# HGRN: who forms the second half of the scaled keys, GpSimd or VectorE

## The reference

```
def _gla_chunked(q, k, v, logf, s0):
    '''S_t = diag(f_t) S_{t-1} + k_t v_t^T, o_t = S_t^T q_t; q,k,logf [B,H,L,dk], v [B,H,L,dv].'''
    c = HGRN_CHUNK
    q, k, v, logf = (_chunks(t, c) for t in (q, k, v, logf))
    gc = jnp.cumsum(logf, axis=-2)
    ...
    attn = jnp.einsum('nbhid,nbhjd,nbhijd->nbhij', q, k, decay)
    ...
        o = qd_i @ s + a_i @ v_i
        s = s * gl_i[..., None] + jnp.einsum('bhcd,bhce->bhde', kd_i, v_i)
```

## Time and profile before

| | before |
|---|---|
| runs | 1703.83, 1696.02, 1699.45 us |
| median | 1699.45 us |
| time of the profiled execution | 1695.34 us |
| span of its profile | 1693.5 us, TensorE clock 0.921 of full speed in the mean |
| HGRN stage, state update ahead of it to the last one in it | 653 to 839 us |

### The profile page before, as it was taken

The page is one execution under the profiler, slowest core; times in us unless marked ns, Lnnn a source line. Parts: engine busy times, 40 slices in busy tenths (PEclk is TensorE's granted clock), DMA queues, the critical chain, the costliest instruction groups (busy, mean ns, idle before and its releaser), DMA issues. The chain is left out here.

```text
span 1693.5 us, 21841 instructions
## 1 busy us (share of the span) xinstructions
PE 1483.8 (88%) x8370; PEld 1087.4 (64%) x8370; DVE 727.8 (43%) x1234; ACT 424.3 (25%) x788; POOL 313.8 (19%) x395
## 2 busy tenths in 40 slices
PE   4999999996999997778679649788999999999955
PEld 1566876754898885444435534476888888888721
DVE  2612670166655654666752630343322222222246
ACT  3111000215555553333232000133221222122101
POOL 0100000103212111344310211101111111111154
PEclk9989789897999998899877769889999999999989
DMA  9624532000930000000010041015999999999877
GB/s 349 204 75 149 151 98 75 25 1 11 376 149 1 1 1 1 8 11 1 1 71 0 0 188 69 0 44 205 393 390 379 378 381 399 383 392 379 276 282 302
DMA packets 100256, 279.48 MB, mean 165 GB/s; under 512 B 22129, under 2 KB 38771, under 8 KB 98908
## 3 DMA queue, kind: packets, MB, share of 16 engines
q1 hardware_dynamic: 84348, 235.27, 37.9%
q0 software_dynamic: 15840, 43.28, 6.6%
HBM read 230.69 MB, written 64.52 MB: 174 GB/s over the span
## 5 line engine op out<-in xcount | busy, mean ns | idle before, releaser
L2313 PEld LDWEIGHTS PS<-arena 128*128 128x128 f32 x2240 | 259.4, 192 | 42.0 <-issue 21.0
L2313 PE MATMUL PS<-arena 128*128 128x128 f32 x2240 | 262.6, 275 | 5.1 <-DMA arena<-in_exp_w_down 3.8
L656 PE MATMUL PS<-arena 128*128 128x512 f32 x384 | 173.5, 606 | 1.5 <-DVE arena L1069 1.5
L2619 DVE TENSOR_SCALAR arena<-PS,arena 128x1024 f32<-128x1024 f32 x70 | 89.9, 1284 | 141.5 <-PE PS L2321 141.5
L2321 PE MATMUL PS<-arena 128*128 128x512 f32 x280 | 137.8, 614 | 0.8 <-DVE arena L2612 0.8
L656 PEld LDWEIGHTS PS<-arena 128*128 128x128 f32 x384 | 73.1, 195 | 86.2 <-issue 85.2
L2612 DVE TENSOR_TENSOR arena<-arena,PS 128x128 f32<-128x128 f32 x70 | 20.1, 288 | 182.5 <-ACT arena L2808 182.5
L2808 ACT ACTIVATE arena<-PS 128x128 f32<-128x128 f32 x70 | 19.4, 278 | 312.3 <-PE PS L2313 312.3
L1009 PEld LDWEIGHTS PS<-arena 64*128 64x128 f32 x640 | 46.7, 208 | 69.4 <-DVE arena L1436 27.8
L668 PE MATMUL PS<-arena 128*128 128x256 f32 (+1 forms) x400 | 90.2, 393 | 0.0
L1009 PE MATMUL PS<-arena 64*128 64x128 f32 x640 | 60.9, 320 | 29.7 <-POOL arena L1848 18.9
(11 more groups left out here) (440 smaller groups left out, 2309.1 us busy)
## 6 DMA issues: line engine op xcount, KB each, us to landing
arena<-in_exp_w_gate SPq DMA_DIRECT2D x70, 512.0 KB, 6.1
arena<-in_exp_w_up SPq DMA_DIRECT2D x70, 512.0 KB, 12.7
arena<-in_exp_w_down SPq DMA_DIRECT2D x70, 512.0 KB, 16.7
y_rows<-arena SPq DMA_DIRECT2D x70, 512.0 KB, 17.1
y_rows<-cst SPq DMA_DIRECT2D x1, 21504.0 KB, 57.7
arena<-in_w_in SPq DMA_DIRECT2D x16, 1024.0 KB, 6.1
arena<-in_w_mod SPq DMA_DIRECT2D x32, 512.0 KB, 3.6
arena<-in_w_mod SPq DMA_DIRECT2D x4, 2048.0 KB, 14.9
```

Of the source, the lines that this page charges most:

```text
L656: pe.matmul(PS[:, b0, :], w[:, k, i * P:(i + 1) * P], hT[:, k, 0:SMP], start=(k == 0), stop=(k == KT - 1))
L2313: mm = pe.matmul(PS[:, bank, 0:P], w[:, k, :], xT[j % 2][:, k, :], start=k == 0, stop=k == KT - 1)
L2619: dve.tensor_scalar(yb[j].rearrange("p (h n) -> p h n", h=2), PS[:, 4 + 2 * (j % 2):6 + 2 * (j % 2), :], gate_col[j % 2], None, ALU.mult). ...
```

## The change

The second half (`pt` = 1) of the scaled keys leaves POOL. DVE forms it by one instruction of 128x896 behind the state updates of the unit before, ahead of `norm_means` or the reciprocal where those follow. A new semaphore `h_ke1` tells of its end; PE waits for it too ahead of r = 1, and ACT ahead of overwriting `hkT`.

```
-                    for pt in range(2):
-                        i = pool.tensor_tensor(hKE[:, pt], spread(hkT[:, P * pt:P * pt + P], 1, LV), hE[u % 2][:, pt, 0:LV, :], ALU.mult)
-                    i.then_inc(h_ke, 1)
+                    pool.tensor_tensor(hKE[:, 0], spread(hkT[:, 0:P], 1, LV), hE[u % 2][:, 0, 0:LV, :], ALU.mult).then_inc(h_ke, 1)
...
+                def hgrn_second_keys(u):
+                    dve.wait_ge(h_kTs, u + 1)
+                    dve.tensor_tensor(hKE[:, 1], spread(hkT[:, P:2 * P], 1, LV), hE[u % 2][:, 1, 0:LV, :], ALU.mult).then_inc(h_ke1, 1)
+
                 for pt in range(2):
                     hgrn_queries(0, pt)
+                hgrn_second_keys(0)
...
                     i.then_inc(h_staken, 1)
+                    if u + 1 < len(UNITS):
+                        hgrn_second_keys(u + 1)
                     if u in (4, 7):
...
                             pe.wait_ge(h_ke, u + 1)
+                            pe.wait_ge(h_ke1, u + 1)
...
                         act.wait_ge(h_ke, u)
+                        act.wait_ge(h_ke1, u)
```

More of the change, by code:

```diff
@@ L427, in trunk_program @@
         hlt, hkt, hkT, hkd = (scratch("u2", 256) for _ in range(4))
-        (h_lt, h_kt, h_x, h_xa, h_kT, h_e, h_ek, h_kTs, h_qe, h_ke, h_kd, h_lvl, h_merge, h_o, h_st, h_otaken,
-         h_staken) = (sem("h_" + n) for n in "lt kt x xa kT e ek kTs qe ke kd lvl merge o st otaken staken".split())
+        (h_lt, h_kt, h_x, h_xa, h_kT, h_e, h_ek, h_kTs, h_qe, h_ke, h_ke1, h_kd, h_lvl, h_merge, h_o, h_st, h_otaken,
+         h_staken) = (sem("h_" + n) for n in "lt kt x xa kT e ek kTs qe ke ke1 kd lvl merge o st otaken staken".split())
         norm_row = small(3 * HD).rearrange("p (m n) -> p m n", m=3)
```

## The result

Nine runs of the changed kernel have a median of 1711.67 us (1708.36 to 1713.61), nine of the kernel before one of 1699.0 us (1696.02 to 1705.22). The ratio is 1.0068, 95% interval 1.0052 to 1.0084: slower by 0.68%.

The account below looks back on a forecast made before the run. TensorE sets the pace between boundaries; at each, r = 1 waits for keys and state updates. Terms -0.4 + 3.4 + 2.0 + 2.0 gave +7.0 us, with 1.5 for the clock +8.5: 1707.9 us, range 1702 to 1712.

Parts of the forecast that it names:

- What bounds it: TensorE's wait ahead of r = 1: of 1.56 us a boundary only 0.53 can be had from faster keys.
- Duration and place of the new instruction: VectorE's second keys, 128x896, take 1.06 us and start behind the state updates, at 685.34 in ordinary units.
- ordinary boundary: Units 1, 2, 4, 6, 7 and 9: r = 1 starts 0.56 us later each, 3.4 us in six.
- Unit 0: First unit: second keys end at 668.1 instead of 668.4, behind L1852's turn, -0.4 us; new instruction about 1.6 us.
- Unit 3: Second keys collide with GpSimd's norm_squares, so r = 1 starts at 723.9 instead of 721.90: +2.0 us.
- Units 5 and 8: norm_means behind the new instruction starts 0.98 us later, delaying ScalarE's root and TensorE's exponents: 2.0 us for both.
- The clock: Low 1.2 GHz level behind TensorE's waits: one more slow stretch, in unit 3, +1.5 us; other changes cancel.
- (b): Rival: more low-clock stretches, unit 4's and a longer one in 3, 5 or 8: +10 to +13 us; chance 0.15.
- (c): Rival: VectorE's second queries take their turn before GpSimd's first keys at the boundaries: -0.6 us, 1698.8; chance 0.08.
- (d): Rival: state updates run undisturbed and the new instruction hides: up to -5 us, 1694.5; chance 0.04.

Follow-up runs that it names:

- no_second_keys: Kernel before without the second half of the scaled keys; TensorE takes the first half for both, so HGRN's result differs: 1693.4 us, ratio 0.9963.
- squares_behind_keys: Changed kernel, but GpSimd's norm_squares of unit 3 waits for the second keys of that unit: 1707.0 us, ratio 1.0054.
- keys_behind_norm: Changed kernel with the second keys moved behind norm_means and the reciprocal instead of ahead of them: 1708.4 us, ratio 1.0057.
- fill_after: Changed kernel with four unused TensorE products of 128x256 ahead of the waits for r = 1 in units 1 to 9: 1696.8 us, ratio 0.9983.
- fill_before: Kernel before with three unused TensorE products of 128x256 ahead of the waits for r = 1 in units 1 to 9: 1692.5 us, ratio 0.9942.
- queries_first: Changed kernel, but GpSimd's first keys wait for VectorE's second queries: 1703.4 us, ratio 1.0018.
- level0_first_gpsimd: Kernel before, all keys on GpSimd, second half in two instructions, level 0 first; r = 1 waits only for level 0: 1697.9 us, ratio 0.9970.

## Why the prediction was right in its mechanism and short in one term

**What bounds it: right.** Of the 1.56 us the prediction gave 0.53 to faster keys, since the state updates come last but one; `no_second_keys` shows 0.43, has the wait for the state updates left, and gains 6 us, not 18.

**Duration and place of the new instruction: right.** 1.09 us measured for 1.06 taken, 0.64 us at the ordinary boundary for 0.56. **Unit 0: right**, the second keys took 1.60 us there for "about 1.6", and r = 1 stands 0.4 us earlier against the start of the stage (670.14 - 655.10 = 15.0 us instead of 668.45 - 653.06 = 15.4). **Unit 3: right**, 1.92 us for 2.0, and `squares_behind_keys` shows its cause. The turn by whole instructions is also what the Trainium skill says in SBUF — State Buffer, section Who interferes with whom; the collisions shown here agree with it (3.06 us for queries of 1.21, 2.37 and 1.66 us for keys of 1.09). **Units 5 and 8: right**, 0.92 us for 0.98, and `keys_behind_norm` takes them back.

Summed from the trace after: -0.4 + 6 x 0.64 + 1.92 + 2 x 0.92 = 7.2 us of direct waits. The prediction had 7.0.

**The clock: mis-sized, and this is the step that made the forecast short.** I wrote that I add one stretch, 1.5 us, and let the rest cancel. The traces show 7.9 us: 15.1 of the stage less 7.2, and the matmul records of the stage took 7.9 us more as well. Low time rose by 19 us, and `fill_after` puts a price of 0.34 us on each, 6.5 us, the rest being within the two digits of the clock. Seven of nine boundaries at the low level should have told me that the remaining two might follow behind longer waits; and the low stretches behind units 5 and 8 grew as well, behind unit 5 from 6.6 us (0.50 from 754.0 to 760.6) to 10 (0.50 from 762.9 to 772.9). I took the price of one stretch and let the others cancel without a reason. The rival (b), to which I gave 0.15, is what happened: +10 to +13 us. That 1711.67 still lies in the range is due to the range, which took in most of (b), and not to the sum. `fill_before` tells the same of the kernel before: some 6 to 10 us of its time were the clock's and not on my list.

The chances leaned the wrong way as well, if only a little: I gave 0.50 to within half a per cent and 0.46 to slower by more; 0.68% with the lower end at 0.52% is slower by more. With 7 us for the clock the sum would have been +14 us against the 15.1 of the traces and the 12.7 of the medians.

**The rivals (c) and (d).** The order of turns did not turn over by itself: the second queries took 3.05 to 3.08 us at all nine boundaries. Nor would it have ended on the other side. Turned over by hand (`queries_first`) the kernel is at 1.0018 to before, +3.1 us, where (c) had -0.6. At the boundary shown it costs 5.20 - 5.05 = +0.15 us where I had worked out -0.15, because GpSimd's first keys ended 3.47 us behind the start of the queries where (c) had 3.16, and so L1860, for which (c) let the second keys wait 0.4 us, held them up for 0.57 (1.66 us instead of 1.09). And the stage is 7.0 us longer than before (192.9 to 185.9), of which 13 us more of low time at 0.34 make 4.4: the clock again, which (c) had left out. (d) needed state updates 1.1 us shorter; they took 1.15 us with and without the keys beside them.

**Open:** why the clock fell behind most waits of 1.56 us and held behind others of the same length (units 3 and 4 before, unit 3 of `fill_after`), and why it differs between executions of `level0_first_gpsimd` and of `no_second_keys`.

## What to carry to other kernels

When a wait names one releaser, look for the next one behind it before pricing what is to be gained: here two thirds of it belonged to the state updates. Moving half of an instruction pair from GpSimd to VectorE did not let the two run side by side where both were ready at once (both read two SBUF operands here), and it puts the moved half behind everything in VectorE's own order. And where TensorE runs in bursts, price each wait twice, once as a wait and once by the slower matmuls behind it; a few unused matmuls in a wait that cannot be removed may give back more than work on the wait itself, as they did in both kernels here. Keep them well below the length of the wait: at the low clock three of them took 2.93 us instead of 1.56 and became the wait.

## What the runs showed of the hardware that I had not expected

TensorE's clock fell to 1.2 GHz behind waits as short as 1.56 us between bursts (in `level0_first_gpsimd` behind waits of 1.13 us, six of nine windows at 0.56 to 0.69), and the added loss weighed as much as the added waits: 7.9 us against 7.2. Four unused products of 128x256 in each of nine waits, 2.0 us for the four, raised the mean clock of the stage from 0.84 to 0.96 and made the kernel 15 us faster. For this kernel it repeats: two profiles of the changed kernel have stages of 201.0 us both.
